# Even layer's output projection with whole float32 operands in place of high and low parts

## The chip, the cores and the metric

The kernel runs on one core of a Trainium2 chip, as one launch. The metric is the device time in microseconds (us), the median of several runs. A core has five engines with a queue of instructions each, worked off in order: PE (TensorE, matrix products), ACT (ScalarE), DVE (VectorE), POOL (GpSimd) and SP (SyncE, which here only starts transfers). They wait for one another through semaphores.

## What is computed

The reference is a two-layer encoder trunk over 256 tokens with 1024 features. The even layer is a mixer with two kinds of attention (8 heads each) and a dense SwiGLU; the odd layer has differential attention and 8 experts. The change touches one product in the even layer:

```python
o = jnp.concatenate([o_a.reshape(B, S, H_A * V_A), o_b.reshape(B, S, H_B * DH_B)], axis=-1)
return o @ w_out          # (256 x 1024) @ (1024 x 1024), float32, then added to the residual h
```

`o_a` (512 columns) is what the latent attention gives, `o_b` (512 columns) what the sparse attention gives.

## The kernel before

Tokens are in two blocks of 128 (`b` = 0, 1), features in chunks of 128. Weights are loaded by SP as tiles of 1 MB, `raw` (128 partitions x 2048 floats; for the output projection 4 chunks x 512 columns), into a ring of `RAW` = 7 slots. The tiles are numbered in the order of their use: 0 to 11 the input projections, 12 to 15 (`T_OUT0` and on) the even layer's output projection, 16 and on (`T_FFN`) the even layer's SwiGLU, and later the odd layer and the experts.

No large product is taken in float32 directly. A weight tile is split: ACT copies it to `w_hi` in the format float32r (fp32r in the rows), DVE writes the rest, `raw - w_hi`, to `w_lo`, both rings of `HL` = 3 slots. The left operand is split too (`fill_o` on ACT and on DVE). PE then makes three float32r products for each chunk: hi x hi and lo x hi in `with_hi` (lines 1796 and 1797), hi x lo in `with_lo` (line 1801). One such product with 512 columns is a *pass* in this text. Other products, attention's and the transposes among them, take float32 operands as they are.

The output projection is 2 halves of the features x 2 token blocks `b` x 2 halves `q` of the output columns x 4 chunks = 32 chunk products. `out_half(layer, half, b, q)` makes four of them as a generator that yields in three pieces of four passes: chunks 0 and 1 with w_hi, chunks 2 and 3 with w_hi, all four with w_lo.

The even attention is a loop of 35 steps on PE, ACT and DVE, written out by hand (`attend_even`), and each engine has a function `beside_even(i)` that puts other work beside step `i`. Steps 0 to 15 score the latent attention's heads, 16 to 31 the sparse attention's, two heads at each even step (line 2057); a step then transposes the probabilities of two steps before (line 2064) and multiplies those of three steps before with the values (line 2073). On PE one piece of a dense product stands beside most steps: input projections to step 16, then the twelve pieces of the first half of the output projection (`out0_first`) at steps 17 to 24, 26, 28, 30 and 32, and the first pieces of the second half (`out0_last`) at 33 and 34. ACT splits the tiles 12 to 15 in quarters beside steps 8 to 11, 12 to 15, 18 to 21 and 26 to 29; DVE follows beside 12 to 15, 21 to 24, 25 to 28 and 30 to 33. DVE also picks the top 64 keys in `top_k` rounds up to step 23.

After the loop, PE finishes the second half for `b` = 0, transposes the last operand block (`fill_o(0, 1, 1)`, line 2091), makes `b` = 1, `q` = 0, transposes the new x of block 0 (line 1837), makes `b` = 1, `q` = 1 and enters the SwiGLU (`first_unit`). DVE adds the results to x (`add_out`), and POOL's clearing of a table in device memory (`slot_rows<-zeros`, 11 transfers of 512 KB) waits for the first of these adds.

SP loads tile i into a slot as soon as tile i - 7 has been split (`lo_ready`). ACT may write `w_hi` for tile i when tile i - 3 has been multiplied (`tile_used`).

Of the kernel before, what the change touches and what calls it, by code (L numbers as in the profile page):

```python
# [27 lines left out]
P = 128  # L28
S, D = 256, 1024
T = S // P  # L30
# [30 lines left out]
AHEAD = 3  # L61
E_STEPS = D_FF_E // 512
# [47 lines left out]
def trunk(nc, a):  # L110
    x_in, consts_in, rope_in, out = a["x"], a["consts"], a["rope"], a["out"]
    with ExitStack() as ctx:
# [55 lines left out]
        ob_hi = at("ob_hi", qk_at, [P, 4, S], F32R)  # L168
        ob_lo = at("ob_lo", qk_at + 4096, [P, 4, S], F32R)
# [222 lines left out]
        def _(sp):  # L392
# [16 lines left out]
            def load(j, e, wanted, last=False):  # L409

                gate_w = a["od_w_gate_e"][0, bass.ds(e, 1)].rearrange("o (c p) f -> p (o c) f", p=P)
                up_w = a["od_w_up_e"][0, bass.ds(e, 1)].rearrange("o (c p) f -> p (o c) f", p=P)
                down_w = a["od_w_down_e"][0, bass.ds(e, 1)].rearrange("o (c p) f -> p (o c) f", p=P)
                for n in range(E_STEPS + 1):
                    g, u, d = job_tiles(n)
                    srcs = [gate_w[:, 4 * k:4 * k + 4, 512 * n:512 * n + 512] for k in range(len(g))]
                    srcs += [up_w[:, 4 * k:4 * k + 4, 512 * n:512 * n + 512] for k in range(len(u))]
                    srcs += [down_w[:, 4 * m:4 * m + 4, 512 * k:512 * k + 512] for m, pair in d for k in range(len(pair))]
                    for i, src in zip(g + u + [i for m, pair in d for i in pair], srcs):
                        if i in wanted:  # L420
# [5 lines left out]
                            sp.wait_ge(lo_ready, j * JOB + T_MOE + i - RAW + 1)  # L426
                            sp.dma_start(slot(raw, s, 4, 512), src).then_inc(raw_landed[s], 16)
# [40 lines left out]
        def _(act):  # L468
            act.dma_start(gain_rows[G_MIX0:G_MIX0 + 8, :], a["ev_norm_mix"][0].rearrange("(c p) -> c p", p=P)).then_inc(mix_landed, 16)

            def hi_part(i, size=None):

                size = size_of[i] if size is None else size
                act.wait_ge(raw_landed[i % RAW], 16 * (i // RAW + 1))
                if i >= HL:
                    act.wait_ge(tile_used, i - HL + 1)
                act.activation(w_hi[:, i % HL, 0:size], raw[:, i % RAW, 0:size], ACT.Copy).then_inc(hi_ready, 1)  # L477

            def hi_piece(i, c):
# [5 lines left out]
                part = act.activation(w_hi[:, i % HL, n * c:n * c + n], raw[:, i % RAW, n * c:n * c + n], ACT.Copy)  # L485
# [16 lines left out]
            def job_hi(j, i):  # L502
# [4 lines left out]
                act.activation(w_hi[:, g % HL, :], raw[:, g % RAW, :], ACT.Copy).then_inc(hi_ready, 1)  # L507
# [172 lines left out]
            def beside_even(i):  # L680
# [18 lines left out]
                hi_pieces(i, [(11, 4), (T_OUT0, 8), (T_OUT0 + 1, 12), (T_OUT0 + 2, 18), (T_OUT0 + 3, 26)])  # L699
# [357 lines left out]
        def _(dve):  # L1057
# [8 lines left out]
            def lo_part(i):  # L1066

                size = size_of[i]
                dve.wait_ge(hi_ready, i + 1)
                dve.tensor_tensor(w_lo[:, i % HL, 0:size], raw[:, i % RAW, 0:size], w_hi[:, i % HL, 0:size].bitcast(F32),  # L1070
                                  ALU.subtract).then_inc(lo_ready, 1)

            def lo_piece(i, c):

                n = size_of[i] // 4
                if c == 0:
                    dve.wait_ge(hi_ready, i + 1)
                part = dve.tensor_tensor(w_lo[:, i % HL, n * c:n * c + n], raw[:, i % RAW, n * c:n * c + n],
                                         w_hi[:, i % HL, n * c:n * c + n].bitcast(F32), ALU.subtract)
# [16 lines left out]
            def job_lo(j, i):  # L1096

                g = T_MOE + i
                dve.wait_ge(hi_ready, j * JOB + g + 1)
                dve.tensor_tensor(w_lo[:, g % HL, :], raw[:, g % RAW, :], w_hi[:, g % HL, :].bitcast(F32), ALU.subtract)\  # L1100
# [58 lines left out]
            def fill_o(layer, half, b):  # L1159

                hi, dst = ((xt_hi, xt_lo), (ob_hi, ob_lo), (oc_hi, oc_lo), (ob_hi, ob_lo))[2 * layer + half]
                hi, dst = hi[:, 0:4, b * P:b * P + P].bitcast(F32), dst[:, 0:4, b * P:b * P + P]
                src = B[o_bank(layer, half, b)].rearrange("p (c t) -> p c t", c=4)
                dve.wait_ge(o_filled_hi, 4 * layer + 2 * half + b + 1)
                if layer:
                    dve.scalar_tensor_tensor(dst, src, gains[:, G_SUB:G_SUB + 1], hi, ALU.mult, ALU.subtract).then_inc(o_filled_lo, 1)
                else:
                    dve.tensor_tensor(dst, src, hi, ALU.subtract).then_inc(o_filled_lo, 1)
# [165 lines left out]
            def beside_even(i):  # L1334
# [20 lines left out]
            fill_o(0, 1, 1)  # L1355
# [90 lines left out]
            def attend_odd(half, beside):  # L1446

                for i in range(H + 3):
# [34 lines left out]
                    if i == 10:  # L1483
# [5 lines left out]
                        else:  # L1489
                            dve.tensor_copy(z[:, 1, 768:1024], B[5][:, 0:256]).then_inc(o_out, 1)  # L1490
                            fill_o(1, 1, 0)
# [48 lines left out]
            fill_o(1, 0, 0)  # L1540

            def beside_second(i):
# [5 lines left out]
                elif i == 4:  # L1548
                    fill_o(1, 0, 1)
# [15 lines left out]
            fill_o(1, 1, 1)  # L1565
# [4 lines left out]
            def first_lo_piece(c):  # L1570

                g, part = T_MOE, slice(512 * c, 512 * c + 512)
                if c == 0:
                    dve.wait_ge(hi_ready, g + 1)
                one = dve.tensor_tensor(w_lo[:, g % HL, part], raw[:, g % RAW, part], w_hi[:, g % HL, part].bitcast(F32), ALU.subtract)
# [211 lines left out]
        def _(pe):  # L1787
# [15 lines left out]
            def hi_of(i, c, width, c0=0, n=None):  # L1803

                n = width if n is None else n
                return w_hi[:, i % HL, c * width + c0:c * width + c0 + n]

            def lo_of(i, c, width, c0=0, n=None):

                n = width if n is None else n  # L1810
                return w_lo[:, i % HL, c * width + c0:c * width + c0 + n]
# [29 lines left out]
            def in_half(q, half):  # L1841
# [3 lines left out]
                if tile:  # L1845
                    pe.wait_ge(hi_ready, tile + 1)
# [13 lines left out]
                pe.wait_ge(lo_ready, tile + 1)  # L1860
# [8 lines left out]
            def out_half(layer, half, b, q):  # L1869

                tile = (T_OUT0, T_OUT1)[layer] + 2 * half + q
                o_hi, o_lo = ((xt_hi, xt_lo), (ob_hi, ob_lo), (oc_hi, oc_lo), (ob_hi, ob_lo))[2 * layer + half]
                pe.wait_ge(o_filled_lo, 4 * layer + 2 * half + b + 1)
                pe.wait_ge(hi_ready, tile + 1)
                bank = B[out_bank(layer, b, q)]
# [5 lines left out]
                pe.wait_ge(lo_ready, tile + 1)  # L1881
# [16 lines left out]
            def first_unit(tile, base, added, n_added):  # L1898

                for b in range(T):  # L1900
                    for k in range(2):
                        pe.wait_ge(hi_ready, tile + k + 1)
# [5 lines left out]
                        pe.wait_ge(lo_ready, tile + k + 1)  # L1908
# [9 lines left out]
            def qkv_half(k, half):  # L1918

                tile = T_QKV + 2 * k + half  # L1920
                pe.wait_ge(hi_ready, tile + 1)
# [7 lines left out]
                pe.wait_ge(lo_ready, tile + 1)  # L1929
# [164 lines left out]
            def out0_first():  # L2094

                left, right = ([out_half(0, 0, b, q) for b in range(T)] for q in range(2))
# [38 lines left out]
            def out0_last():  # L2135

                for q in range(2):
                    yield from out_half(0, 1, 0, q)
# [7 lines left out]
            all_of(out_half(0, 1, 1, 0))  # L2146
            pe.wait_ge(x_added, 2)
            fill_block(0)
            all_of(out_half(0, 1, 1, 1))

            def ffn_products(tiles, bank, w, by_block=False):

                per = KC // len(tiles)
                for k, i in enumerate(tiles):
                    pe.wait_ge(hi_ready, T_FFN + i + 1)
# [7 lines left out]
                    pe.wait_ge(lo_ready, T_FFN + i + 1)  # L2163
# [19 lines left out]
            for n in range(FFN_STEPS):  # L2183
# [16 lines left out]
                if d:  # L2200
                    pe.wait_ge(f_tlo, 2 * n)
                    for half, i in enumerate(d):
                        pe.wait_ge(hi_ready, T_FFN + i + 1)
# [7 lines left out]
                        pe.wait_ge(lo_ready, T_FFN + i + 1)  # L2211
# [11 lines left out]
            pe.wait_ge(lo_ready, tile + 1)  # L2223
# [93 lines left out]
            def out1_first():  # L2317

                for b in range(T):
                    for q in range(2):  # L2320
                        yield from out_half(1, 0, b, q)
# [17 lines left out]
            all_of(out_half(1, 1, 0, 0))  # L2339
            fill_o(1, 1, 1)  # L2340
            all_of(out_half(1, 1, 0, 1))
            all_of(out_half(1, 1, 1, 0))
            pe.wait_ge(x_added, 6)
            fill_block(0)
            last_half = out_half(1, 1, 1, 1)
# [70 lines left out]
            def job(j, last=False):  # L2416
                def products(tiles, bank, first=False):
                    for k, i in enumerate(tiles):
# [3 lines left out]
                        pe.wait_ge(hi_ready, j * JOB + g + 1)  # L2422
# [3 lines left out]
                        pe.wait_ge(lo_ready, j * JOB + g + 1)  # L2426
# [14 lines left out]
                for n in range(E_STEPS + 1):  # L2441
# [16 lines left out]
                    for s, pair in d:  # L2458
# [3 lines left out]
                        for half, i in enumerate(pair):  # L2462
                            k = T_MOE + i
                            pe.wait_ge(hi_ready, j * JOB + k + 1)
# [3 lines left out]
                            pe.wait_ge(lo_ready, j * JOB + k + 1)  # L2468
# [109 lines left out]
```

## Time and profile before

| what | value |
|---|---|
| time, median of 3 runs (1398.68 to 1398.83) | 1398.7 us |
| span of the profiled execution, first to last instruction | 1396.7 us |
| PE busy | 1386.0 us, 99% |
| DVE busy, ACT busy | 1141.3 us (82%), 987.6 us (71%) |
| mean granted TensorE clock | 0.998 of full speed |
| HBM traffic | 439.5 MB, mean 315 GB/s |

The profiled execution has no time of its own beside its span; what lies around the span is the 2.0 us between 1396.7 and the median of the runs. Matmuls overlap in the profile: the duration of one is longer than the distance to the next, so the distance between starts tells what a matmul costs, not its duration. A float32 matmul is recorded as two matmuls, each with a weight load of its own; transposes and float32r matmuls are recorded as one.

### The profile page before, as it was taken

Reading aid. Unit: us, or ns where it says so; the run is one execution under the profiler, and the core shown is the slowest. Engines: PE = TensorE matmul, PEld = TensorE weight load, DVE = VectorE, ACT = ScalarE, POOL = GpSimd, SP = SyncE. Lnnn points to the kernel's source line nnn. Section 1 sums busy time; section 2 is a strip of 40 time slices with the busy share of each in tenths; the row PEclk is TensorE's granted clock in tenths of the full one; section 3 lists DMA queues with packets and bytes.
Section 4 is the critical chain, followed back from the end, with each engine's and each line's share of the span. In section 5 each row is a group of like instructions: output and inputs, shape, how many; then the busy total and the mean of one; then the engine's idle time right before and its main releaser. Section 6 shows DMA issues by size and latency. Waiting matters only on the chain.

```text
span 1396.7 us, 18564 instructions
## 1 busy us (share of the span) xinstructions
PE 1386.0 (99%) x6628; PEld 1149.5 (82%) x6628; DVE 1141.3 (82%) x1110; ACT 987.6 (71%) x968; POOL 80.7 (6%) x105
## 2 busy tenths in 40 slices
PE   9999999999999999999999999999999999999997
PEld 8878888888878888888888888888888888888886
DVE  6786555566787988888888898888889889888997
ACT  7676543346677777877877877787787778778776
POOL 2012000002116200000000000000000000001100
PEclk9999999999999999999999999999999999999999
DMA  9427755555335999999999999999999999999994
GB/s 340 161 92 265 268 197 189 181 181 178 125 104 211 382 387 386 389 388 387 389 388 387 376 389 387 384 372 388 387 367 388 387 363 384 388 366 381 390 387 151
DMA packets 218544, 440.16 MB, mean 315 GB/s; under 512 B 7407, under 2 KB 11681, under 8 KB 218497
## 3 DMA queue, kind: packets, MB, share of 16 engines
q1 hardware_dynamic: 214000, 424.61, 84.0%
q0 software_dynamic: 3472, 11.27, 2.2%
q10 hardware_dynamic: 1024, 3.67, 0.6%
q8 instruction: 27, 0.44, 0.1%
q14 instruction: 21, 0.16, 0.0%
HBM read 426.93 MB, written 12.59 MB: 315 GB/s over the span
## 4 chain that ended last, share of the span: by engine, by line
PE 97%; DVE 1%; DMA 0%; ACT 0%; issue 0%; DVEq 0%; SPq 0%
PE bank L1801 30%; PE bank L1796 30%; PE bank L1797 29%; PE bank L2438 2%; PE bank L1992 1%; PE bank L2073 1%; PE bank L2064 0%; PE bank L2398 0%; PE bank L2263 0%; PE bank L2049 0%; PE bank L1837 0%; DMA x_sb<-in_x_dram 0%; PE bank L2180 0%; PE bank L2057 0%; PE bank L1790 0%; PE bank L1792 0%
## 5 line engine op out<-in xcount | busy, mean ns | idle before, releaser
L1100 DVE TENSOR_TENSOR w_lo<-raw,w_hi 128x2048 fp32r<-128x2048 f32 x335 | 758.0, 2289 | 86.8 <-ACT w_hi L507 86.3
L507 ACT ACTIVATE w_hi<-raw 128x2048 fp32r<-128x2048 f32 x336 | 642.9, 1919 | 145.8 <-PE bank L1801 143.5
L1796 PE MATMUL bank<-w_hi,xg_hi 128*128 128x512 f32 x896 | 351.0, 392 | 0.0
L1797 PE MATMUL bank<-w_hi,xg_lo 128*128 128x512 f32 x896 | 348.8, 389 | 0.0
L1801 PE MATMUL bank<-w_lo,xg_hi 128*128 128x512 f32 x896 | 240.1, 390 | 0.1
L1796 PE MATMUL bank<-w_hi,ht_hi 128*128 128x512 f32 x528 | 206.3, 391 | 0.0
L1797 PE MATMUL bank<-w_hi,ht_lo 128*128 128x512 f32 x528 | 205.6, 389 | 0.0
L1801 PEld LDWEIGHTS bank<-w_lo,xg_hi 128*128 128x128 f32 x896 | 167.9, 188 | 36.5 <-DVE w_lo L1100 1.4
L1797 PEld LDWEIGHTS bank<-w_hi,xg_lo 128*128 128x128 f32 x896 | 168.3, 188 | 34.2
L1796 PEld LDWEIGHTS bank<-w_hi,xg_hi 128*128 128x128 f32 x896 | 168.3, 188 | 34.1
L1070 DVE TENSOR_TENSOR w_lo<-raw,w_hi 128x2048 fp32r<-128x2048 f32 (+4 forms) x52 | 114.5, 2211 | 43.7 <-ACT w_hi L477 42.8
L477 ACT ACTIVATE w_hi<-raw 128x2048 fp32r<-128x2048 f32 (+4 forms) x52 | 96.6, 1862 | 73.6 <-PE bank L1801 73.3
L1796 PE MATMUL bank<-w_hi,xt_hi 128*128 128x512 f32 (+3 forms) x384 | 146.9, 387 | 0.0
L1797 PE MATMUL bank<-w_hi,xt_lo 128*128 128x512 f32 (+3 forms) x384 | 142.7, 376 | 0.0
L1801 PE MATMUL bank<-w_lo,ht_hi 128*128 128x512 f32 x528 | 139.6, 389 | 0.0
L1801 PEld LDWEIGHTS bank<-w_lo,ht_hi 128*128 128x128 f32 x528 | 99.1, 188 | 20.7
L1797 PEld LDWEIGHTS bank<-w_hi,ht_lo 128*128 128x128 f32 x528 | 99.2, 188 | 20.4
L1796 PEld LDWEIGHTS bank<-w_hi,ht_hi 128*128 128x128 f32 x528 | 99.2, 188 | 20.3
L1801 PE MATMUL bank<-w_lo,xt_hi 128*128 128x512 f32 (+3 forms) x384 | 92.0, 379 | 0.1
L1796 PEld LDWEIGHTS bank<-w_hi,xt_hi 128*128 128x128 f32 x384 | 72.4, 188 | 12.8 <-issue 0.6
L1797 PEld LDWEIGHTS bank<-w_hi,xt_lo 128*128 128x128 f32 x384 | 72.4, 188 | 11.2
L1801 PEld LDWEIGHTS bank<-w_lo,xt_hi 128*128 128x128 f32 x384 | 68.4, 188 | 12.5 <-DVE w_lo L1070 0.5
(341 smaller groups left out, 1055.1 us busy)
## 6 DMA issues: line engine op xcount, KB each, us to landing
raw<-in_od_w_gate_e_dram SPq DMA_DIRECT2D x112, 1024.0 KB, 9.0
raw<-in_od_w_up_e_dram SPq DMA_DIRECT2D x112, 1024.0 KB, 9.2
raw<-in_od_w_down_e_dram SPq DMA_DIRECT2D x112, 1024.0 KB, 9.6
raw<-in_od_w_qkv_dram SPq DMA_DIRECT2D x12, 1024.0 KB, 5.2
raw<-in_ev_w_gate_dram SPq DMA_DIRECT2D x11, 1024.0 KB, 5.2
raw<-in_ev_w_up_dram SPq DMA_DIRECT2D x11, 1024.0 KB, 5.0
raw<-in_ev_w_down_dram SPq DMA_DIRECT2D x11, 1024.0 KB, 5.0
raw<-in_ev_w_in_dram SPq DMA_DIRECT2D x6, 1024.0 KB, 15.1
```

Source lines behind the costliest of these rows:

```text
L477: act.activation(w_hi[:, i % HL, 0:size], raw[:, i % RAW, 0:size], ACT.Copy).then_inc(hi_ready, 1)
L507: act.activation(w_hi[:, g % HL, :], raw[:, g % RAW, :], ACT.Copy).then_inc(hi_ready, 1)
L1070: dve.tensor_tensor(w_lo[:, i % HL, 0:size], raw[:, i % RAW, 0:size], w_hi[:, i % HL, 0:size].bitcast(F32), ALU.subtract).then_inc(lo_read ...
L1100: dve.tensor_tensor(w_lo[:, g % HL, :], raw[:, g % RAW, :], w_hi[:, g % HL, :].bitcast(F32), ALU.subtract)\
L1796: pe.matmul(out_ap, l_hi, r_hi, start=first, stop=False)
L1797: pe.matmul(out_ap, l_lo, r_hi, start=False, stop=False)
L1801: return pe.matmul(out_ap, l_hi, r_lo, start=False, stop=last)
L1992: m = pe.transpose(B[turn_bank(G)][0:parts, k * P:k * P + P], ap, ident)
L2073: m = pe.matmul(B[7][:, DH * h:DH * h + DH], pt[:, v % 2, k, :], z[:, k, v0 + DH * h:v0 + DH * h + DH], start=(k == 0), stop=(k == b))
L2438: m = pe.transpose(B[h_bank(n)][:, c * P:c * P + P], hh[:, n % 2, c * P:c * P + P], ident)
```

## The change

The tiles 12 to 15 are no longer split and neither is the operand. ACT copies the transposed operand once, as float32 (`oa_t`, `ob_t`), and DVE's `fill_o` for this layer is gone. PE multiplies the raw tile with it in float32: `out0_half` has one matmul for a chunk where `out_half` had three, and yields after chunk 0, after chunk 1 and at the end, so its three pieces have 1, 1 and 2 matmuls. The number of pieces and the steps that they stand at stay as they are. As `lo_ready` no longer comes for these tiles, SP loads tiles 19 to 22 when tiles 12 to 15 have been multiplied (`tile_used`). `split(i)` counts the tiles that are split before tile i, and the slots of `w_hi` and `w_lo` and the counts of `hi_ready` and `lo_ready` go by it everywhere. The odd layer's projection keeps the old form (`out1_half`).

```diff
+WHOLE = range(T_OUT0, T_OUT0 + 4)
+def split(i):
+    return i - sum(w < i for w in WHOLE)
...
+        oa_t = at("oa_t", xt_at, [P, 4, S])
+        ob_t = at("ob_t", qk_at, [P, 4, S])
...
-                if i >= RAW:
-                    sp.wait_ge(lo_ready, i - RAW + 1)
+                if i - RAW in WHOLE:
+                    sp.wait_ge(tile_used, i - RAW + 1)
+                elif i >= RAW:
+                    sp.wait_ge(lo_ready, split(i - RAW) + 1)
...
             def fill_o(layer, half, b):
-                dst = (xt_hi, ob_hi, oc_hi, ob_hi)[2 * layer + half]
+                dst = (oa_t, ob_t, oc_hi, ob_hi)[2 * layer + half]
...
-                hi_pieces(i, [(11, 4), (T_OUT0, 8), (T_OUT0 + 1, 12), (T_OUT0 + 2, 18), (T_OUT0 + 3, 26)])
+                hi_pieces(i, [(11, 4)])
...
-                elif i == 16:
-                    fill_o(0, 0, 0)
-                elif i == 21:
-                    fill_o(0, 0, 1)
-                elif i == 32:
-                    fill_o(0, 1, 0)
-                lo_pieces(i, [(10, 4), (11, 8), (T_OUT0, 12), (T_OUT0 + 1, 21), (T_OUT0 + 2, 25), (T_OUT0 + 3, 30)])
+                lo_pieces(i, [(10, 4), (11, 8)])
             attend_even(beside_even)
-            fill_o(0, 1, 1)
...
+            def out0_half(half, b, q):
+                tile = T_OUT0 + 2 * half + q
+                o_t = (oa_t, ob_t)[half]
+                pe.wait_ge(o_filled_hi, 2 * half + b + 1)
+                pe.wait_ge(raw_landed[tile % RAW], 16 * (tile // RAW + 1))
+                bank, w = B[out_bank(0, b, q)], raw[:, tile % RAW, :]
+                for c in range(4):
+                    m = pe.matmul(bank[:, :], o_t[:, c, b * P:b * P + P], w[:, 512 * c:512 * c + 512],
+                                  start=(half == 0 and c == 0), stop=(half == 1 and c == 3))
+                    if c < 2:
+                        yield
+                if b == 1:
+                    m.then_inc(tile_used, 1)
+                elif half == 1:
+                    m.then_inc(out_done, 1)
+                yield
```

## Rows read from the trace of the kernel before

**Rows 1.** The page: busy time by engine; the chain that ended last, by engine.

```profile
PE 1386.0 (99%) x6628; PEld 1149.5 (82%) x6628; DVE 1141.3 (82%) x1110; ACT 987.6 (71%) x968; POOL 80.7 (6%) x105
...
PE 97%; DVE 1%; DMA 0%; ACT 0%; issue 0%; DVEq 0%; SPq 0%
```

**Rows 2.** Busy time in the attention loop's second half, granted clock in the seventh column.

```profile
core 0: us, PE busy (x) PEld busy (x) DVE busy (x) ACT busy (x) POOL busy (x), PEclk, DMA share, GB/s
86.00:114.70 28.70, 28.68 (x182) 22.07 (x181) 23.78 (x80) 19.79 (x65) 0.00 (x0) 1.00 0.34 111
```

**Rows 3.** Timeline of PE, steps 28 and 29: start, duration, instruction.

```profile
109.19 0.70 PE L2057 MATMUL bank<-kb_t,qb_t 64*128 64x256 f32 x4
109.83 0.44 PE L2064 MATMUL bank<-cst,pr 128*128 128x128 f32 x2
110.10 0.56 PE L2073 MATMUL bank<-z,pt 128*128 128x64 f32 x4
110.47 0.48 PE L1796 MATMUL bank<-w_hi,xt_hi 128*128 128x512 f32 x1
110.78 0.39 PE L1797 MATMUL bank<-w_hi,xt_lo 128*128 128x512 f32 x1
111.01 0.39 PE L1796 MATMUL bank<-w_hi,xt_hi 128*128 128x512 f32 x1
...
111.48 0.38 PE L2064 MATMUL bank<-cst,pr 128*128 128x128 f32 x2
```

**Rows 4.** Timeline of PE, from step 33 to the SwiGLU, cut.

```profile
114.70 0.48 PE L1796 MATMUL bank<-w_hi,ob_hi 128*128 128x512 f32 x1
...
124.75 0.48 PE L1796 MATMUL bank<-w_hi,ob_hi 128*128 128x512 f32 x1
...
127.57 0.39 PE L1796 MATMUL bank<-w_hi,xt_hi 128*128 128x512 f32 x1
```

**Rows 5.** Windows of PE: the transposes inside that stretch, and the whole.

```profile
118.94:119.29 0.35, 0.35 (x5) 1.00 1.05 410
...
123.97:124.75 0.78, 0.78 (x9) 1.00 1.05 389
...
sum 12.87, PE 12.87; mean PE 2.57
```

**Rows 6.** Timeline of PE near the end: two float32 products (L2490), the last three records apart.

```profile
1387.16 0.39 PE L2487 MATMUL bank<-y_lo,sel_t 128*128 128x512 f32 x1
1387.39 1.93 PE L2490 MATMUL bank<-y,sel_t 128*128 128x512 f32 x4
...
1387.87 1.45 PE L2490 MATMUL bank<-y,sel_t 128*128 128x512 f32 x3
```

**Rows 7.** Waits of PE's weight loads, 86 to 114.7 us: total, times, longest.

```profile
PEld bank L2064 <- issue: 0.7, 2, 0.3
PEld bank L2064 <- ACT pr L676: 0.7, 2, 0.3
```

**Rows 8.** The largest gap of that stretch in PE's timeline.

```profile
92.77 0.27 PE L2064 MATMUL bank<-cst,pr 128*128 128x128 f32 x1
93.06 0.41 PE L2073 MATMUL bank<-z,pt 128*128 128x64 f32 x2
```

**Rows 9.** Groups of ACT and DVE that split weights and operand.

```profile
L485 ACT ACTIVATE w_hi<-raw x4: 613/618/620, 105.2 to 109.7; 128x512 fp32r<-128x512 f32 x4
L1078 DVE TENSOR_TENSOR w_lo<-raw,w_hi x10: 682/686/691, 100.4 to 114.6; 128x512 fp32r<-128x512 f32 x10
L1168 DVE TENSOR_TENSOR ob_lo<-bank,ob_hi x2: 691/692/692, 113.4 to 120.2; 128x512 fp32r<-128x512 f32 x2
```

**Rows 10.** SP's starts of the loads of tiles 20 and 21, 22 and 23.

```profile
103.73 5.01 SPq L407 DMA_DIRECT2D raw<-in_ev_w_gate_dram  x2
115.28 0.37 SPq L407 DMA_DIRECT2D raw<-in_ev_w_up_dram  x1
124.35 0.37 SPq L407 DMA_DIRECT2D raw<-in_ev_w_up_dram  x1
```

**Rows 11.** Loads of 1 MB started at 131.4 us: time to landing.

```profile
raw<-in_ev_w_down_dram SPq DMA_DIRECT2D x1, 1024.0 KB, 12.5
```

**Rows 12.** Timeline of ACT: the splits of tiles 20 and 21, and of 22.

```profile
143.67 3.71 ACT L477 ACTIVATE w_hi<-raw 128x2048 fp32r<-128x2048 f32 x2
...
150.52 1.93 ACT L477 ACTIVATE w_hi<-raw 128x2048 fp32r<-128x2048 f32 x1 [3.14 <-PE bank L1801]
```

More of the change, by code:

```diff
@@ L476, in hi_part @@
                     act.wait_ge(tile_used, i - HL + 1)
-                act.activation(w_hi[:, i % HL, 0:size], raw[:, i % RAW, 0:size], ACT.Copy).then_inc(hi_ready, 1)
+                act.activation(w_hi[:, split(i) % HL, 0:size], raw[:, i % RAW, 0:size], ACT.Copy).then_inc(hi_ready, 1)
             def hi_piece(i, c):
@@ L484, in hi_piece @@
                     act.wait_ge(tile_used, i - HL + 1)
-                part = act.activation(w_hi[:, i % HL, n * c:n * c + n], raw[:, i % RAW, n * c:n * c + n], ACT.Copy)
+                part = act.activation(w_hi[:, split(i) % HL, n * c:n * c + n], raw[:, i % RAW, n * c:n * c + n], ACT.Copy)
                 if c == 3:
@@ L506, in job_hi @@
                 act.wait_ge(tile_used, j * JOB + g - HL + 1)
-                act.activation(w_hi[:, g % HL, :], raw[:, g % RAW, :], ACT.Copy).then_inc(hi_ready, 1)
+                act.activation(w_hi[:, split(g) % HL, :], raw[:, g % RAW, :], ACT.Copy).then_inc(hi_ready, 1)
             counts = {"squares": 0, "var": 0}
@@ L1068, in lo_part @@
                 size = size_of[i]
[L1069 to L1070 removed]
+                dve.wait_ge(hi_ready, split(i) + 1)
+                dve.tensor_tensor(w_lo[:, split(i) % HL, 0:size], raw[:, i % RAW, 0:size], w_hi[:, split(i) % HL, 0:size].bitcast(F32),
                                   ALU.subtract).then_inc(lo_ready, 1)
@@ L1076, in lo_piece @@
                 if c == 0:
-                    dve.wait_ge(hi_ready, i + 1)
-                part = dve.tensor_tensor(w_lo[:, i % HL, n * c:n * c + n], raw[:, i % RAW, n * c:n * c + n],
-                                         w_hi[:, i % HL, n * c:n * c + n].bitcast(F32), ALU.subtract)
+                    dve.wait_ge(hi_ready, split(i) + 1)
+                part = dve.tensor_tensor(w_lo[:, split(i) % HL, n * c:n * c + n], raw[:, i % RAW, n * c:n * c + n],
+                                         w_hi[:, split(i) % HL, n * c:n * c + n].bitcast(F32), ALU.subtract)
                 if c == 3:
@@ L1098, in job_lo @@
                 g = T_MOE + i
-                dve.wait_ge(hi_ready, j * JOB + g + 1)
-                dve.tensor_tensor(w_lo[:, g % HL, :], raw[:, g % RAW, :], w_hi[:, g % HL, :].bitcast(F32), ALU.subtract)\
+                dve.wait_ge(hi_ready, j * JOB + split(g) + 1)
+                dve.tensor_tensor(w_lo[:, split(g) % HL, :], raw[:, g % RAW, :], w_hi[:, split(g) % HL, :].bitcast(F32), ALU.subtract)\
                    .then_inc(lo_ready, 1)
@@ L1573, in first_lo_piece @@
                 if c == 0:
-                    dve.wait_ge(hi_ready, g + 1)
-                one = dve.tensor_tensor(w_lo[:, g % HL, part], raw[:, g % RAW, part], w_hi[:, g % HL, part].bitcast(F32), ALU.subtract)
+                    dve.wait_ge(hi_ready, split(g) + 1)
+                one = dve.tensor_tensor(w_lo[:, split(g) % HL, part], raw[:, g % RAW, part], w_hi[:, split(g) % HL, part].bitcast(F32),
+                                        ALU.subtract)
                 if c == 3:
@@ L1845, in in_half @@
                 if tile:
-                    pe.wait_ge(hi_ready, tile + 1)
+                    pe.wait_ge(hi_ready, split(tile) + 1)
                 for b in range(T):
@@ L1859, in in_half @@
                             yield
-                pe.wait_ge(lo_ready, tile + 1)
+                pe.wait_ge(lo_ready, split(tile) + 1)
                 for b in range(T):
@@ L1867, in in_half, with out1_half @@
                     yield
[L1869 to L1875, printed above, removed]
+            def out0_half(half, b, q):
[14 more added lines that the diff above has]
+                yield
+            def out1_half(half, b, q):
+                tile = T_OUT1 + 2 * half + q
+                o_hi, o_lo = ((oc_hi, oc_lo), (ob_hi, ob_lo))[half]
+                pe.wait_ge(o_filled_lo, 2 * half + b + 1)
+                pe.wait_ge(hi_ready, split(tile) + 1)
+                bank = B[out_bank(1, b, q)]
                 for c in range(4):
@@ L1880, in out_half @@
                         yield
-                pe.wait_ge(lo_ready, tile + 1)
+                pe.wait_ge(lo_ready, split(tile) + 1)
                 for c in range(4):
@@ L1901, in first_unit @@
                     for k in range(2):
-                        pe.wait_ge(hi_ready, tile + k + 1)
+                        pe.wait_ge(hi_ready, split(tile + k) + 1)
                         for c in range(4):
@@ L1907, in first_unit @@
                                     hi_of(tile + k, c, 512), kc == 0)
-                        pe.wait_ge(lo_ready, tile + k + 1)
+                        pe.wait_ge(lo_ready, split(tile + k) + 1)
                         for c in range(4):
@@ L1920, in qkv_half @@
                 tile = T_QKV + 2 * k + half
-                pe.wait_ge(hi_ready, tile + 1)
+                pe.wait_ge(hi_ready, split(tile) + 1)
                 for b in range(T):
@@ L1928, in qkv_half @@
                             yield
-                pe.wait_ge(lo_ready, tile + 1)
+                pe.wait_ge(lo_ready, split(tile) + 1)
                 for b in range(T):
@@ L2094, in out0_first @@
             def out0_first():
-                left, right = ([out_half(0, 0, b, q) for b in range(T)] for q in range(2))
+                left, right = ([out0_half(0, b, q) for b in range(T)] for q in range(2))
                 for pieces, n in ((left[0], 3), (right[0], 2), (left[1], 3), (right[0], 1), (right[1], 3)):
@@ L2137, in out0_last @@
                 for q in range(2):
-                    yield from out_half(0, 1, 0, q)
+                    yield from out0_half(1, 0, q)
             ahead_last = out0_last()
@@ L2222, in _ @@
             tile = T_QKV - 1
-            pe.wait_ge(lo_ready, tile + 1)
+            pe.wait_ge(lo_ready, split(tile) + 1)
             for b in range(T):
```

57 lines of the change are left out of this document (27 added, 30 removed).

## Prediction

> **What bounds the kernel.** I read the page first: PE is busy 99% of the span and makes 97% of the chain that ended last [rows 1]. As matmul durations overlap, that alone proves little, so I went to PE's timeline and measured distances between starts. In the attention loop's second half the windows show PE without idle time at a granted clock of 1.00, that is 2.4 GHz, while ACT and DVE have gaps [rows 2]. In the step pair 28 and 29 each instruction starts when the one before has streamed: two passes are 0.23 us apart (110.78 to 111.01), and the first pass of a piece, after short matmuls, takes 0.31 (110.47 to 110.78), so a piece of four passes takes 1.01 us (110.47 to 111.48) [rows 3]. After the loop it is denser still: from 114.70 to 127.57 PE goes through 48 passes of the projection and little else [rows 4]. So what counts is how long PE needs for the projection, and then whether anything that the change moves makes PE wait.
>
> **The price of a float32 product.** The kernel has two float32 products of exactly this shape, 128 x 128 with 512 columns, at line 2490. Four records stand for them. The last three start 1.45 - 0.59 = 0.86 us apart over two distances (0.592 us is the duration of one record), so 0.43 us each; the first distance is 1387.87 - 1387.39 = 0.48 [rows 6]. Thus a product takes 0.86 us, or 0.91 where it opens a piece. Three passes take 3 x 0.228 = 0.68 us: the last twelve of the projection take 127.57 - 124.75 = 2.82 us with an opening of 0.09, so 2.73 / 12 = 0.228 each [rows 4]. A whole float32 product is dearer by 0.18 us, though it is one instruction instead of three. I take 0.86 and 0.91; the bounds are 0.86 for all and 0.91 for all, since the 0.48 may be the mark of a new weight load or of the wait for y just before.
>
> Beside these rows, the Trainium skill has two rules that part ways. FP8 and Floating Point Precision, TensorE Precision Notes, says that true FP32 makes four passes through the array: 4 x 0.213 = 0.85 us at 512 columns, and the rows agree. Perfetto Trace Analysis, Engine Utilization, halves the array's output rate for FP32_LOW_HIGH: read as the price of the whole product this would be 0.43 us, and the rows agree with it only for each of the two records.
>
> **In the loop.** Twelve pieces of the first half stand in steps 17 to 32. Before they cost 12 x 1.01 = 12.1 us, of which step 28 shows one [rows 3]. After, eight of them are one product (0.91) and four are two products (0.48 + 3 x 0.43 = 1.77): 7.3 + 7.1 = 14.4 us. That is **+2.3 us** (+1.7 if every product is 0.86).
>
> Against it stands the PE idle time that the relieved engines can give back. ACT loses 16 quarters of 0.62 us and DVE 16 of 0.69 plus four operand parts of 0.69 [rows 9]: 9.9 and 13.8 us of work. Neither sets the end; this work lies under PE's, so its price is nothing, and its removal is worth only what PE waited for it. The waits of the weight loads show 0.7 us for probabilities from ACT and 0.7 us with no releaser in this stretch [rows 7]; most of it is hidden by the matmul still streaming. In the timeline I compared each distance with the same group in undisturbed steps. About seven stand out, together 0.5 us; the largest is 0.29 us from 92.77 to 93.06, where a single transpose takes 0.11 elsewhere [rows 8]. Bounds are 0 and 1.4 us; I take **-0.5 us**. A shorter step can't open much of a new wait: the pair 28 and 29 falls from about 2.9 to 2.8 us, and the scores made at its start are wanted, as probabilities, a whole pair later.
>
> **Behind the loop.** The stretch of 12.87 us [rows 4, 5] holds, beside the projection, the last values product (0.36), the operand transposes (0.35) and the x transposes (0.78) [rows 5]: 1.49 us. The other 11.38 us are 48 passes x 0.228 = 10.9 and four openings of 0.09. After, 16 products x 0.86 = 13.8 and four openings of 0.05 make 14.0: **+2.6 us** (13.8 to 14.6 by the bounds, so +2.4 to +3.2). The waits in it have cover. The last operand block now needs only ACT's copy (0.60 us, without DVE's 0.69 behind it), and three products, 2.6 us, lie between its transposes and its first use. DVE's two additions before x is transposed are covered by the four products of `b` = 1, `q` = 0 (3.4 us instead of 2.7). In `first_unit` the order and the distances stay.
>
> **The sum.** +2.3 - 0.5 + 2.6 = **+4.4 us**, and nothing further down takes it back, since PE stays the bound there. In the profiled execution the span goes from 1396.7 to 1401.1; with the 2.0 us around it that is 1403.1, and the same 4.4 us on the median of 1398.7 gives 1403.1 (+0.3%). With the bounds: +1.7 - 1.4 + 2.4 = +2.7 at the least, and all products at 0.91 without idle regained at the most: 32 x 0.91 = 29.1 less 23.5 (12.1 + 11.4) = +5.6.
>
> **The transfers that move.** SP's wait for tiles 19 to 22 changes from the split to the use. Before, tiles 20 and 21 started at 103.7 and 108.4, tile 22 at 115.3 and tile 23 at 124.35 [rows 10]. After, tile 19 starts at about 104 (step 24), 20 at 116 (step 32), 21 at about 127.8 and 22 at 132.0, with 23, which is queued behind it on SP and was free at about 128, directly after. They then run beside the clearing of the table, when a load takes up to 12.5 us to land [rows 11]. ACT wants tile 20 at 143.7 + 4.4 = 148.1, tile 21 one split of 1.9 us later, at 149.9, and tile 22 at 150.5 + 4.4 = 154.9 [rows 12]. So tile 21 has 22 us and tile 22 has 23 us, and two more megabytes in that crowded stretch cost some 5 us more: 12.5 + 5 = 18. I cost it at nothing; without that margin each us that a tile is late is a us of PE.
>
> **Rivals.**
>
> *The passes are hidden after all (little change).* If more of PE's time in the loop than I see is waiting, the dearer products fill it and only the tail pays. For it: matmul ends are modelled, and 1.4 us of waits are listed [rows 7]. Against it: the steps are alike to 0.01 us where PE streams [rows 3]. It gives +2.3 - 2.5 + 2.6 = +2.4, 1401.1 us, and is under the 0.2% line (2.8 us, about what a measurement of this kernel can tell from no change).
>
> *The float32 product is cheap (faster).* If a product of this shape took one record's time, 0.43 us, the projection would fall from 23.5 to 32 x 0.43 + 0.8 = 14.6 us: -8.9, 1389.8 us. The sign turns where a product costs less than 23.5 / 32 = 0.73 us. Against it: four records for two products [rows 6]. In the Trainium skill this is the rule of Perfetto Trace Analysis, Engine Utilization, named above.
>
> *A late tile (much slower).* Tile 21 or 22 lands after ACT wants it. For it: the starts move by 19 and 17 us into the stretch where transfers are crowded [rows 10, 11]. Against it: the margin of 22 us. With landings of 30 us PE would stand still for some 8 us: +12, 1411 us.
>
> **How the numbers follow.** The forecast, +2.8 to +5.6 with 4.4 inside, has a chance of 0.83; hidden passes 0.06; cheap product 0.04; late tile 0.05; 0.02 is left for what I don't see, in either direction. The predicted time is 1403.1. The likeliest case alone reaches from 1401.5 to 1404.3; with a margin for a partly late tile or more idle regained I give 1401.2 to 1404.9. Slower by over 0.2%: 0.83 + 0.05 + 0.01 = 0.89. Within: 0.06. Faster: 0.05.
>
> **What the profile after would show.** In the timeline, `out0_half` records in pairs 0.43 us apart, 64 of them; pieces of 0.91 and 1.77 us in the loop, so that steps 19, 24, 26 and 32 grow by 0.75 and the others shrink by 0.1. The first SwiGLU pass at about 132.0 instead of 127.57, and everything behind it shifted by the same amount. ACT and DVE busy 10 and 14 us less. PE's clock still 1.00. The prediction is wrong if the distance of the records isn't 0.43, if the wait list shows PE or ACT waiting for `raw` between 145 and 165 us, or if the shift at 127.57 isn't the shift of the end.

## The result and the profile after

The changed kernel takes 1404.58 us (median of 4 runs, 1404.34 to 1404.76) against 1398.69 us (4 runs, 1398.55 to 1398.83). The ratio is 1.0043 with a 95% interval of 1.0029 to 1.0057, so it is slower by 5.9 us (4.1 to 8.0). The forecast was 1403.1 us, +4.4; the measured time lies inside the range given, 1401.2 to 1404.9, near its upper end. The profiled execution took 1404.34 us with a span of 1402.1, which is 5.4 us over the 1396.7 of before.

Busy time by engine, and the chain that ended last, from the page of the changed kernel, to be held against [rows 1]:

```profile
PE 1390.1 (99%) x6596; PEld 1141.8 (81%) x6596; DVE 1129.6 (81%) x1090; ACT 980.0 (70%) x952; POOL 84.1 (6%) x105
...
PE 97%; DVE 1%; DMA 0%; ACT 0%; issue 0%; SPq 0%; DVEq 0%
```

PE has 32 records fewer (96 passes went, 32 products of two records came) and is busy 4.1 us more. DVE lost 11.7 us and ACT 7.6 us net, and the share of PE in the chain is the same, as it should be if the work that went lay under PE's; relief, below, tests that.

PE's timeline of the changed kernel at steps 28 and 29 (start, duration, instruction) answers to [rows 3]. Lines 2076, 2083 and 2092 are what 2057, 2064 and 2073 were; 1878 is the float32 product:

```profile
107.82 0.70 PE L2076 MATMUL bank<-kb_t,qb_t 64*128 64x256 f32 x4
108.45 0.44 PE L2083 MATMUL bank<-cst,pr 128*128 128x128 f32 x2
108.73 0.56 PE L2092 MATMUL bank<-z,pt 128*128 128x64 f32 x4
109.12 1.08 PE L1878 MATMUL bank<-raw,oa_t 128*128 128x512 f32 x2
110.03 0.38 PE L2083 MATMUL bank<-cst,pr 128*128 128x128 f32 x2
```

A piece of one product takes 110.03 - 109.12 = 0.91 us, as forecast. But the values product before it now takes 109.12 - 108.73 = 0.39 us, where it took 0.37 in [rows 3]: ahead of a float32r piece the last short matmul was recorded 0.02 to 0.03 us shorter, ahead of a float32 piece it is not. So the 0.09 us that a float32r piece's first pass takes longer was partly paid back just before it, and taking these 0.02 to 0.03 us into account, an opening costs 0.06 us in either form.

The same timeline behind the loop answers to [rows 4]:

```profile
117.00 1.08 PE L1878 MATMUL bank<-raw,ob_t 128*128 128x512 f32 x2
...
128.25 1.04 PE L1838 MATMUL bank<-cst,x_sb 128*128 128x128 f32 x8
129.12 3.60 PE L1878 MATMUL bank<-raw,ob_t 128*128 128x512 f32 x8
132.16 0.80 PE L1797 MATMUL bank<-w_hi,xt_hi 128*128 128x512 f32 x1
132.79 0.40 PE L1798 MATMUL bank<-w_hi,xt_lo 128*128 128x512 f32 x1
```

The last piece of four products runs from 129.12. The SwiGLU's first pass is recorded at 132.16 and its second not 0.23 but 0.63 us later. That distance looked like a stall of 0.4 us at first; two experiments below show that it is none.

To compare stages I take one stretch in every kernel, from the first scores of step 16 to the transposes of x block 1, which follow the SwiGLU's first twelve passes. The two ends in the kernel before, from PE's timeline:

```profile
87.05 0.38 PE L2057 MATMUL bank<-kb_t,qb_t 64*128 64x128 f32 x2
...
130.30 0.49 PE L1837 MATMUL bank<-cst,x_sb 128*128 128x128 f32 x3
```

and in the changed kernel:

```profile
86.79 0.49 PE L2076 MATMUL bank<-kb_t,qb_t 64*128 64x128 f32 x4
...
135.33 1.03 PE L1838 MATMUL bank<-cst,x_sb 128*128 128x128 f32 x8
```

It is 43.25 us long before and 48.54 after: **+5.29 us**. From there the shift stays through the odd layer and most of the experts: the same product of the expert stage (first rows gathered) starts at 435.6 before and 440.7 after. One step of 0.4 us comes late in the experts; it has a section of its own below. The stretch is a better measure of what the products cost than the total, because its start moves by up to 1 us between the kernels (86.75 to 87.80), although PE has the same work before it in all of them.

How the stage lengths came out in all kernels:

| kernel | start | end | length | against before |
|---|---|---|---|---|
| before | 87.05 | 130.30 | 43.25 | |
| changed | 86.79 | 135.33 | 48.54 | +5.29 |
| relief | 86.91 | 130.17 | 43.26 | +0.01 |
| late_loads | 87.33 | 130.59 | 43.26 | +0.01 |
| first_half | 86.75 | 132.54 | 45.79 | +2.54 |
| second_half | 86.83 | 132.85 | 46.02 | +2.77 |
| one_pass | 87.20 | 119.20 | 32.00 | -11.25 |
| inter | 86.87 | 136.32 | 49.45 | +6.20 |
| grouped | 87.16 | 136.61 | 49.45 | +6.20 |
| evened | 87.23 | 136.14 | 48.91 | +5.66 |
| coarse32 | 87.18 | 135.85 | 48.67 | +5.42 |
| coarse32_late | 87.80 | 136.54 | 48.74 | +5.49 |
| coarse | 86.99 | 130.94 | 43.95 | +0.70 |
| coarse_late | 87.13 | 131.20 | 44.07 | +0.82 |

### The profile page after: what moved, and what is told of

Same layout as the page of the kernel before. It is cut to its first block, busy times and chain, and to the rows that moved or that the text cites. A ratio compares the mean times of both kernels' runs of the same rounds, so it can differ in the third digit from the quotient of the medians.

```text
span 1402.1 us, 18459 instructions
## 1 busy us (share of the span) xinstructions
PE 1390.1 (99%) x6596; PEld 1141.8 (81%) x6596; DVE 1129.6 (81%) x1090; ACT 980.0 (70%) x952; POOL 84.1 (6%) x105
## 4 chain that ended last, share of the span: by engine, by line
PE 97%; DVE 1%; DMA 0%; ACT 0%; issue 0%; SPq 0%; DVEq 0%
PE bank L1802 29%; PE bank L1797 29%; PE bank L1798 29%; PE bank L1878 2%; PE bank L2457 2%; PE bank L2011 1%; PE bank L2092 1%; DMA raw<-in_ev_w_in_dram 0%; PE bank L2083 0%; PE bank L2417 0%; PE bank L2282 0%; PE bank L2068 0%; PE bank L1838 0%; PE bank L2199 0%; PE bank L2076 0%; PE bank L1791 0%
## 5 line engine op out<-in xcount | busy, mean ns | idle before, releaser
L1797 PE MATMUL bank<-w_hi,xt_hi 128*128 128x512 f32 (+3 forms) x368 | 140.4, 386 | 0.8 <-ACT w_hi L578 0.8
L1798 PE MATMUL bank<-w_hi,xt_lo 128*128 128x512 f32 (+3 forms) x368 | 136.4, 375 | 0.0
L1802 PE MATMUL bank<-w_lo,xt_hi 128*128 128x512 f32 (+3 forms) x368 | 87.3, 377 | 0.1
L1797 PEld LDWEIGHTS bank<-w_hi,xt_hi 128*128 128x128 f32 x368 | 69.3, 188 | 13.6 <-ACT w_hi L578 1.0
L1798 PEld LDWEIGHTS bank<-w_hi,xt_lo 128*128 128x128 f32 x368 | 69.3, 188 | 11.1 <-issue 0.2
```

Of the source, the lines that this page charges most:

```text
L1797: pe.matmul(out_ap, l_hi, r_hi, start=first, stop=False)
L1798: pe.matmul(out_ap, l_lo, r_hi, start=False, stop=False)
L1802: return pe.matmul(out_ap, l_hi, r_lo, start=False, stop=last)
```

## Experiments

### Relief without the dearer products (relief)

```diff
-        oa_t = at("oa_t", xt_at, [P, 4, S])
-        ob_t = at("ob_t", qk_at, [P, 4, S])
+        oa_t = at("oa_t", xt_at, [P, 4, S], F32R)
+        ob_t = at("ob_t", qk_at, [P, 4, S], F32R)
...
-                bank, w = B[out_bank(0, b, q)], raw[:, tile % RAW, :]
-                for c in range(4):
+                bank, w = B[out_bank(0, b, q)], w_hi[:, 2, :]
+                for k in range(12):
+                    c = (k // 2) if k < 8 else k - 8
...
-                    if c < 2:
+                    if k in (3, 7):
                         yield
```

> The staging of the changed kernel (no splits on ACT and DVE, late loads), but each product as three float32r passes as before, in pieces of four; the passes read a w_hi slot instead of the real weights, so the projection's values are wrong and only its timing counts. Theory A (PE is the bound and never waited for the removed work): the stretch from the first sparse scores (87.05 us before) to the first SwiGLU pass (127.57) stays 40.5 us within 0.1, total 1398.7 +- 0.4. Rival B (my prediction's term: the relieved engines give PE 0.5 us): 40.0 us, total 1398.2. Rival C (what went beyond the forecast, 1.5 us, comes from the later loads or the new counts of the rings): the total is above 1399.5, with waits behind the projection.

Measured: 1399.08 us, ratio 1.0005 (0.9995 to 1.0014). The stretch is 43.26 us, 0.01 from the kernel before. The waits of PE's weight loads from 86 to 116 us (total, times, longest) are the ones of [rows 7] to the digit, with ACT and DVE relieved of all the splitting:

```profile
PEld bank L2084 <- issue: 0.7, 2, 0.3
PEld bank L2084 <- ACT pr L686: 0.7, 2, 0.3
```

The windows of that stretch show the relief itself (PE, PEld, DVE, ACT and POOL busy; clock; DMA), first in the kernel before:

```profile
87.05:130.30 43.25, 43.23 (x254) 34.43 (x253) 32.84 (x94) 25.35 (x73) 7.30 (x13) 1.00 0.44 150
```

and in relief:

```profile
86.91:130.17 43.26, 43.24 (x253) 34.44 (x253) 23.15 (x77) 21.08 (x64) 7.31 (x13) 1.00 0.36 122
```

DVE has 9.7 us less to do and ACT 4.3, and PE takes as long as before. So the work that was removed was worth nothing in this stretch, and the 0.5 us that I took off the sum did not exist. Theory A held and B fell. C fell for this stretch and for its size (the total is not above 1399.5), but not wholly: relief has, like the changed kernel, one longer wait in the last experts, see below.

### Later loads alone (late_loads)

```diff
-                if i >= RAW:
+                if i - RAW in range(T_OUT0, T_OUT0 + 4):
+                    sp.wait_ge(tile_used, i - RAW + 1)
+                elif i >= RAW:
                     sp.wait_ge(lo_ready, i - RAW + 1)
```

> The kernel before with one edit: SP starts tiles 19 to 22 when tiles 12 to 15 have been multiplied, as in the changed kernel. Theory A: hidden, 1398.7 +- 0.3 and no PE wait between 140 and 170 us. Rival C (the later loads cost part of the 1.5 us beyond the forecast): +0.5 to +1.5.

Measured: 1398.47 us, ratio 1.000 (0.9991 to 1.001), stretch 43.26 us. Theory A held: the loads are hidden. In the changed kernel itself the load of tile 21, started at 128.4, took this long to land (the issues of that window):

```profile
raw<-in_ev_w_gate_dram SPq DMA_DIRECT2D x1, 1024.0 KB, 14.6
```

and ACT's timeline shows the splits of tiles 20 and 21, then of 22:

```profile
148.69 3.72 ACT L487 ACTIVATE w_hi<-raw 128x2048 fp32r<-128x2048 f32 x2
155.52 1.92 ACT L487 ACTIVATE w_hi<-raw 128x2048 fp32r<-128x2048 f32 x1 [3.11 <-PE bank L1802]
```

Tile 21 landed at 143.0 and was wanted at 148.69 + 1.86 = 150.6. The margin of 22 us that I worked out left 7.5 us when it had landed.

### One half at a time (first_half, second_half)

```diff
-WHOLE = range(T_OUT0, T_OUT0 + 4)
+WHOLE = range(T_OUT0, T_OUT0 + 2)        # first_half
+WHOLE = range(T_OUT0 + 2, T_OUT0 + 4)    # second_half
...
+                if half == X:            # the half that stays split: the three passes of before, o_filled_lo and all
...
+                    return
```

ACT and DVE keep the splits of the other half's tiles and operand at their steps of before.

> Only tiles 12 and 13 and the operand of the latent attention are whole; tiles 14 and 15 and their operand are split as before. Theory A: the loop part pays its 16 products, +2.5 us by the first SwiGLU pass, and nothing at the entry into the SwiGLU, because the last products are float32r again: 1401.2. Rival B (idle PE time is given back in part): +1.8. Rival C (a fixed cost at the entry, whatever is before it): +2.9.

> Only tiles 14 and 15 and the operand of the sparse attention are whole. Theory A: the loop keeps its length, the stretch behind it pays +2.3 us and the entry into the SwiGLU +0.4, together +2.7: 1401.4. Rival (the relief in steps 25 to 33 gives back 0.4): +2.3. The sum of this run and first_half should be the whole change at the first SwiGLU pass, 5.2 us.

Measured: 1400.97 us (ratio 1.0018, 1.0008 to 1.0027) and 1401.1 us (1.0018, 1.0009 to 1.0028). The stretches grew by 2.54 and 2.77 us, and their sum, 5.31, is the whole change (5.29). The cost is additive: it goes with the products, wherever they stand, which speaks for price and against any wait. In first_half that is theory A's +2.5 and neither rival's. In second_half theory A's number (+2.7) held, but the 0.4 us that it put at the entry into the SwiGLU is no cost of its own, as inter shows below.

### One pass instead of four (one_pass)

The edit is relief's, but with the loop `for c in range(4)` of the changed kernel kept: one float32r pass for each product.

> The changed kernel with one float32r pass for each product in place of the float32 matmul (it reads a w_hi slot instead of the weights, so the projection's values are wrong). Theory A: as long as PE is the bound, 32 x (0.86 - 0.23) = 20.2 us less than the changed kernel at the first SwiGLU pass; pieces of one pass take 0.31. Where steps get that short, PE must begin to wait for ACT and DVE; I expect some 5 us of that, so -15 us. Rival (other engines already set the pace of the loop): -8 us or less, all of it behind the loop.

Measured: 1388.28 us (one run), the stretch 32.00 us, 16.5 less than in the changed kernel; theory A expected 15 less. Of the 20.2 us by price 3.7 are missing, by difference, and new waits show in PE's timeline, the longest of them:

```profile
91.53 0.27 PE L2083 MATMUL bank<-cst,pr 128*128 128x128 f32 x1
92.52 0.41 PE L2092 MATMUL bank<-z,pt 128*128 128x64 f32 x2 [0.71 <-DVE o_a L1311]
```

The same spot was the largest gap of before, 0.29 us [rows 8]. PE waits there for DVE to write out the results of the last eight heads. In relief it kept its 0.29 us (92.64 to 92.93) with the splits gone; here, with PE faster, it grew to 0.99. So with PE's need in this stretch cut by 20.2 us, the other engines held it up for 3.7 at the most.

### Is there a stall at the entry into the SwiGLU? (inter, grouped)

```diff
+                    if probe:             # half 1, b = 1, q = 1; inter: after each product, grouped: four after the last
+                        pe.matmul(B[4][:, :], w_hi[:, 0, 0:P], w_hi[:, 0, 0:512], start=True, stop=True)
```

> The changed kernel with four extra float32r passes into a free bank, one after each of the last four float32 products before the SwiGLU. Tests what a change from a float32 product of 512 columns to a float32r pass costs. Theory E (each such change costs 0.4 us on the float32r pass after it, as seen at the entry, 132.16 to 132.79): the four passes add 4 x (0.23 + 0.40) less the 0.40 that was paid once anyway = +2.1 us. Rival (the 0.4 at the entry was a wait for the operand or the weights of the SwiGLU): +0.9 us.

> The same four extra float32r passes, all after the last float32 product. Theory E: one change as in the changed kernel, 4 x 0.23 = +0.9 us, and the 0.63 us distance stands at the first extra pass, no longer at the SwiGLU's first. Rival (a wait for the SwiGLU's operand): the first extra pass takes 0.23, and the SwiGLU's first pass keeps part of the wait or loses it.

Measured (one run each): 1405.03 and 1405.39 us. Both stretches are 49.45 us, 0.91 over the changed kernel: 4 x 0.228. Theory E, my own, fell with inter, for which it said +2.1. (In grouped it said +0.9, and the long distance did move to the first extra pass, 132.52 to 133.16.) PE's timeline of inter shows why I was misled:

```profile
130.29 1.02 PE L1881 MATMUL bank<-raw,ob_t 128*128 128x512 f32 x2
130.75 0.79 PE L1886 MATMUL bank<-w_hi 128*128 128x512 f32 x1
131.38 1.02 PE L1881 MATMUL bank<-raw,ob_t 128*128 128x512 f32 x2
```

A product and a pass take 131.38 - 130.29 = 1.09 us, 0.86 + 0.23. But the pass is recorded 0.46 us after the product's first record, that is beside its second, and its duration is 0.79 instead of 0.39. The distance of 0.63 us at the entry was mostly the last product's own second half. The rival had inter's number, +0.9, but not its reason: extra passes would have filled a wait of 0.4 us at the entry, and the stretch would have grown by 0.5. Nothing waits there.

### What an opening costs (evened, coarse32, coarse32_late)

```diff
-                    if c < 2:
+                    if c < 3:                                     # evened: pieces of one product
+                    if c == 1:                                    # coarse32, coarse32_late: pieces of two
...
-                elif i < 25 or i in (26, 28, 30, 32):
+                elif i < 33:                                      # evened
+                elif i in (17, 18, 20, 22, 24, 26, 28, 30):       # coarse32
+                elif i in (17, 18, 20, 22, 24, 26, 29, 32):       # coarse32_late
```

> The changed kernel with pieces of one product each: the first half's 16 products stand beside steps 17 to 32, one each, instead of pieces of 1, 1 and 2 beside twelve of them. Theory A (each opening costs 0.05 us, PE waits for nobody): four openings more, +0.2 us against the changed kernel, 1404.8. Rival D (uneven steps make PE wait for probabilities and values, which is why no idle time came back): -0.4 us, 1404.2.

> The changed kernel with the first half's 16 float32 products in eight pieces of two (beside steps 17, 18, 20, 22, 24, 26, 28 and 30) instead of twelve pieces. Theory F (a float32 piece costs 0.10 us for its opening beside 0.86 a product, as evened showed with four more): four openings fewer, -0.4 us against the changed kernel from the first sparse scores to the second x transposes (48.54 us). Rival (openings cost 0.05 as forecast): -0.2. Rival (steps without a piece make PE wait): 0 or more.

> As coarse32, but the last two of the eight float32 pieces stand beside steps 29 and 32 instead of 28 and 30, so that PE has a piece just before step 33, where coarse32 waited 0.6 us for ACT's copy of the probabilities. Theory F: the four openings saved now show, 48.54 - 0.4 = 48.1 us from the first sparse scores to the second x transposes. Rival (a step without a piece always makes PE wait, wherever it is): 48.5 or more.

Measured: evened 1405.0 us (4 runs, ratio to before 1.0045, 1.0028 to 1.0062), its stretch 0.37 us over the changed kernel for four openings more; uneven steps were not what held PE up, so rival D fell. Dividing gives 0.09 an opening, but that counts a wait along. At step 27 PE begins the values of the next eight heads and needs DVE's output of the eight before, which ends at 106.11. Two transposes take 106.26 - 105.90 = 0.36 us where 0.22 is the rule:

```profile
105.90 0.38 PE L2083 MATMUL bank<-cst,pr 128*128 128x128 f32 x2
106.26 0.63 PE L2092 MATMUL bank<-z,pt 128*128 128x64 f32 x4
```

The changed kernel has no wait at that place; its step 26 has two products, which leave DVE the time. Without these 0.14 us the four openings cost 0.23, 0.06 each, which is theory A's +0.2. The changed kernel has such a wait eight heads earlier, at step 19 (one transpose, 0.37 us where 0.11 is the rule):

```profile
92.37 0.27 PE L2083 MATMUL bank<-cst,pr 128*128 128x128 f32 x1
92.74 0.41 PE L2092 MATMUL bank<-z,pt 128*128 128x64 f32 x2
```

coarse32 (one run, 1404.58 us) has four openings fewer and yet 0.13 us more, so its second rival held, that steps without a piece make PE wait. In its timeline the transposes of step 33 wait for ACT's copy of the probabilities, as step 32 has no piece:

```profile
115.89 0.56 PE L2092 MATMUL bank<-z,pt 128*128 128x64 f32 x4
116.89 0.41 PE L2083 MATMUL bank<-cst,pr 128*128 128x128 f32 x2 [0.44 <-ACT pt L681]
```

From one to the next are 1.00 us where 0.39 is the rule: 0.61 lost. But the wait of step 19 is gone in coarse32, whose step 18 has two products (94.48 to 94.59 is 0.11), which saves 0.25, and four openings of 0.06 save 0.22: 0.61 - 0.25 - 0.22 = +0.14, measured +0.13. coarse32_late (one run, 1405.32 us) was to cure that wait and did, but opened two of 0.34 us behind steps 28 and 30, which had no piece before the next transposes, the first of them:

```profile
109.30 0.56 PE L2092 MATMUL bank<-z,pt 128*128 128x64 f32 x4
110.03 0.41 PE L2083 MATMUL bank<-cst,pr 128*128 128x128 f32 x2 [0.17 <-ACT pt L681]
```

My 48.1 us was wrong, the measured 48.74 is on the rival's side; by the same terms it is 0.68 - 0.25 - 0.22 = +0.21 over the changed kernel, measured +0.20. So theory F (0.10 us for an opening) fell, and the three kernels agree with the rows: a float32 piece costs 0.06 us to open (a product takes 0.91 in its first place and 0.86 elsewhere), and what goes beyond that in evened and in coarse32 is a wait that comes or goes.

### The same with the kernel before (coarse, coarse_late)

```diff
-                    if c % 2:
+                    if c == 3 or (c == 1 and (layer == 1 or half == 1)):
                         yield
...
-                elif i < 25 or i in (26, 28, 30, 32):
+                elif i in (17, 18, 20, 22, 24, 26, 28, 30):       # coarse
+                elif i in (17, 18, 20, 22, 24, 26, 29, 32):       # coarse_late
```

> The kernel before with the first half's 48 passes in eight pieces (of eight and four passes, beside steps 17, 18, 20, 22, 24, 26, 28 and 30) instead of twelve of four. Theory F (PE is the bound, an opening costs a float32r piece 0.09 us): four openings fewer, -0.35 us, 1398.3, the fastest of all, though too little for the timing to tell. Rival (the light steps make PE wait for probabilities): +0.5 us or more.

> As coarse, with the last two pieces beside steps 29 and 32. Theory F: of coarse's 43.95 us the 0.6 at step 33 goes, 43.3 us remain, level with the kernel before (43.25), since the light steps 19 to 25 still cost what the openings save. Rival (the empty steps 27 and 28 open a new wait as long): 43.9.

Measured: 1399.02 us (ratio 1.0005, 0.9996 to 1.0015) and 1399.31 us (1.0005, 0.9996 to 1.0015). The stretches are 0.70 and 0.82 us longer than before. Both expectations missed, and the rivals held: the openings saved are less than the new waits, most of them for ACT's copies. The old spacing, a piece between any two sets of transposes that have no scores between them, is what keeps PE fed. None of the versions tried that compute the projection beats the kernel before.

### A wait 1150 us further down

One difference lies outside the stretch. In the last experts, DVE computes row numbers (`rows`, a CAST) and then splits a weight tile, and PE waits for this `w_lo`. In the kernel before:

```profile
1280.98 0.17 DVE L1688 CAST rows<-moe_s 128x4 uint32<-128x4 f32 x1
1281.08 6.69 DVE L1100 TENSOR_TENSOR w_lo<-raw,w_hi 128x2048 fp32r<-128x2048 f32 x3
1283.43 1.20 PE L1801 MATMUL bank<-w_lo,xg_hi 128*128 128x512 f32 x4
```

and in the changed kernel:

```profile
1286.04 0.17 DVE L1689 CAST rows<-moe_s 128x4 uint32<-128x4 f32 x1
1286.53 6.70 DVE L1110 TENSOR_TENSOR w_lo<-raw,w_hi 128x2048 fp32r<-128x2048 f32 x3 [0.32 <-issue]
1288.87 1.20 PE L1802 MATMUL bank<-w_lo,xg_hi 128*128 128x512 f32 x4 [0.47 <-DVE w_lo L1110]
```

From the CAST to the split it is 0.49 us instead of 0.10, and PE gets on 0.39 us later. The traces of all kernels show the same split in two: in the eight where all four tiles are whole (changed, relief, one_pass, inter, grouped, evened, coarse32, coarse32_late) the distance is 0.48 or 0.49, in the six others 0.08 to 0.10. So these 0.39 us belong to the change, but not to its products, since relief has them and first_half and second_half don't; nor to the later loads, since late_loads doesn't. Why DVE starts late there stays open: the profile names nothing that it waits for.

## Why the prediction was right, and what was off

**The direction and the mechanism held.** PE is the bound, a float32 product with 512 columns takes two records of 0.43 us, and 32 of them replace 96 passes of 0.228. relief shows that the price of the products is the whole effect in the stretch (0.01 us without it), first_half and second_half that it is additive, and one_pass that taking passes away pays. The clock stayed at 1.00 in the stretch.

That the time fell inside the range owes something to luck: the likeliest case ended at 1404.3, and the margin above it was meant for a partly late tile, which never came. The 5.9 us by the medians are also over the +5.6 that my bounds allowed at the most; the 5.4 of the span are not.

**In the loop** the step that failed is the -0.5 us of PE idle time given back. I had read distances above the common ones as waiting for the engines that the change relieves. relief measures it: 0.0. Part of such distances is fixed (0.09 us more before each set of scores and 0.06 behind it, in every kernel), and the true waits, as the one at 92.77 [rows 8], are for DVE's output of a block, which the splits didn't delay: in relief it is the same 0.29 us. The row of the waits [rows 7] named ACT, but for its place in the chain, not for its load.

**The opening** was mis-sized, by 0.03 us: the sum has 0.05 for a float32 piece against 0.09 for a float32r piece, but the latter's 0.09 comes with a distance 0.02 to 0.03 us shorter just before it, so that both cost 0.06. With twelve pieces the loop then comes to +2.3 + 12 x 0.03 = +2.66; measured from 87.05 and 86.79 to 114.70 and 117.00 it is 30.21 - 27.65 = +2.56.

**Behind the loop** I forecast +2.6. From 114.70 and 117.00 to the second pass of the SwiGLU, 127.80 and 132.79, it is 15.79 - 13.10 = +2.69.

**The sum** was +4.4, measured +5.3 in the stretch: 0.5 from the idle time, 0.3 to 0.4 from openings. The span grew by 5.4: the stretch's 5.29, less the 0.26 that its start came earlier in this execution, and the 0.39 of the wait in the last experts, which no term of the prediction has. I had written that nothing further down takes the cost back; that held, but something further down added to it, and by my own sign (the shift at the entry into the SwiGLU should be the shift of the end) 5.0 there against 5.4 at the end is a miss.

The 0.5 us between the span's 5.4 and the medians' 5.9 I can't place. Medians of the kernel before itself ran from 1398.29 to 1398.69 in the different comparisons, and the interval of the ratio (4.1 to 8.0 us) holds both.

**The rivals.** Hidden passes: excluded by first_half, where the 16 products of the loop cost 2.54 us and none is hidden. A cheap product: excluded by the records. A late tile: the tile landed 7.5 us ahead of its use, and late_loads is level.

## What to carry to other kernels

Where one engine sets the time, count that engine's time for the new form before looking at what the others are spared: here some 19 us less work on two other engines (11.7 and 7.6) were worth nothing, and 0.17 us more for each of 32 products were paid in full. Before taking credit for idle time of the bounding engine, find what the wait is for and whether the removed work stands ahead of it in that engine's queue; a distance that is longer than its neighbours may be the fixed cost of a change of shape. Two ways of writing the same product are best compared by a row of the same shape in the same kernel. And before a difference of two kernels is divided by the number of pieces, the waits that came or went between them have to be taken out.

## What I had not expected of the hardware

A float32r pass behind a float32 product is recorded beside the product's second half (0.46 us after its start, duration 0.79 us), although the two together take 0.86 + 0.23 us, as inter and grouped show: in such places only sums over whole pieces can be trusted. And a float32 piece is no cheaper to open than a float32r piece, 0.06 us either way: the float32r piece's first distance is 0.09 us longer than the others, but the short matmul ahead of it takes 0.37 us for four instead of 0.39, while the float32 piece has 0.05 to 0.06 in its first distance alone.
